# Three transformer blocks on one Trainium2 core: 1/rms moved to GpSimd, and the start of the kernel loaded in quarters

## The reference

```python
def rmsnorm(x, g, eps=1e-6):
    y = x * lax.rsqrt(jnp.mean(x * x, axis=-1, keepdims=True) + eps)
    return y * g

def swiglu(h, w_up, w_down):                 # 1024 -> 2 x 2816 -> 1024
    gate, up = jnp.split(h @ w_up, 2, axis=-1)
    return (jax.nn.silu(gate) * up) @ w_down

# first model, layers i = 0, 1 (the mixer is multiscale pooling, then differential attention)
    x = x + 0.5 * swiglu(rmsnorm(x, norm_g[i, 0]), ffn_w_up[i, 0], ffn_w_down[i, 0])
    h = rmsnorm(x, norm_g[i, 1])
    x = x + mixer(h) @ w_out                 # with attention over the memory, whose k, v come from rmsnorm(mem)
    x = x + 0.5 * swiglu(rmsnorm(x, norm_g[i, 2]), ffn_w_up[i, 1], ffn_w_down[i, 1])
  x = rmsnorm(x, final_norm_g)
# second model, one layer
    mix = mixer2(rms_norm(x, g_pre_mix)) @ w_out          # block attention and retention
    x = x + rms_norm(mix, g_post_mix)
    c = cross_attention(rms_norm(x, g_pre_cross), rms_norm(mem_2, g_mem))
    x = x + rms_norm(c, g_post_cross)
    f = (silu(gate) * up) @ w_down                        # of rms_norm(x, g_pre_ffn)
    x = x + rms_norm(f, g_post_ffn)
```

## Time and profile before

| What | us |
|---|---|
| median of 3 runs (1547.17 to 1547.46) | 1547.34 |
| the profiled execution, its own time | 1548.35 |
| its span, first to last instruction | 1546.6 |
| PE busy, share of the span | 1469.9, 95% |
| DVE busy | 880.9, 57% |
| ACT busy | 723.5, 47% |
| POOL busy | 5.1, 0% |
| DMA, moved 262.07 MB | mean 169 GB/s |

### The profile page before, as it was taken

One profiled execution on the slowest core, in us unless ns is written; L12 is line 12 of the kernel. 1 busy time (PEld: TensorE's weight loads), 2 busy tenths in 40 slices (PEclk: granted clock), 3 DMA queues, 4 the chain that ended last, 5 costly groups with the idle time before them and its releaser, 6 DMA issues.

```text
span 1546.6 us, 18695 instructions
## 1 busy us (share of the span) xinstructions
PE 1469.9 (95%) x7412; PEld 1237.0 (80%) x7412; DVE 880.9 (57%) x1001; ACT 723.5 (47%) x928; POOL 5.1 (0%) x13
## 2 busy tenths in 40 slices
PE   5999998999999999999989899999998899899997
PEld 4888898988888888888876688888877688788886
DVE  4555567655455654546668665445766655555444
ACT  5454453445434644445445555435433643444443
POOL 0000000000000000000000000000000000000000
PEclk9999999999999999999999899999999899999999
DMA  9555553445555455555323355554523353345551
GB/s 384 193 188 184 178 188 118 166 152 204 189 188 183 163 214 190 177 188 182 136 82 109 136 185 204 184 191 161 177 110 109 129 184 136 123 163 190 191 190 55
DMA packets 36846, 262.07 MB, mean 169 GB/s; under 512 B 4096, under 2 KB 4224, under 8 KB 5536
## 3 DMA queue, kind: packets, MB, share of 16 engines
q1 hardware_dynamic: 35568, 254.53, 46.7%
q0 software_dynamic: 1200, 6.42, 1.0%
HBM read 259.88 MB, written 1.05 MB: 169 GB/s over the span
## 4 chain that ended last, share of the span: by engine, by line
PE 85%; DVE 8%; ACT 5%; issue 1%; DMA 1%; DVEq 0%; SPq 0%; ACTq 0%
PE prod L864 14%; PE prod L866 14%; PE prod L865 14%; PE acc L864 9%; PE acc L865 9%; PE acc L866 9%; PE prod L858 4%; PE prod L859 4%; PE prod L860 4%; DVE w_lo L1288 2%; PE aux L894 2%; ACT w_hi L1106 1%; DVE sq L1566 1%; ACT four L1239 1%; DVE small L1372 1%
## 5 line engine op out<-in xcount | busy, mean ns | idle before, releaser
L1288 DVE TENSOR_TENSOR w_lo<-raw,w_hi 128x2048 fp32r<-128x2048 f32 x238 | 544.9, 2291 | 333.8 <-ACT w_hi L1106 333.4
L1106 ACT CAST w_hi<-raw 128x2048 fp32r<-128x2048 f32 x238 | 453.4, 1907 | 233.5 <-PE acc L866 154.7
L864 PE MATMUL prod<-w_hi,acts_h 128*128 128x512 f32 x944 | 376.1, 398 | 16.9 <-DVE w_lo L1288 13.5
L866 PE MATMUL prod<-w_hi,acts_l 128*128 128x512 f32 x944 | 369.5, 391 | 0.0
L865 PE MATMUL prod<-w_lo,acts_h 128*128 128x512 f32 x944 | 368.8, 391 | 0.0
L864 PE MATMUL acc<-w_hi,mix_h 128*128 128x512 f32 x600 | 240.2, 400 | 3.5 <-DVE mix_l L1581 2.5
L865 PE MATMUL acc<-w_lo,mix_h 128*128 128x512 f32 x600 | 235.9, 393 | 0.0
L866 PE MATMUL acc<-w_hi,mix_l 128*128 128x512 f32 x600 | 235.7, 393 | 0.0
L864 PEld LDWEIGHTS prod<-w_hi,acts_h 128*128 128x128 f32 x944 | 178.2, 189 | 54.5 <-DVE w_lo L1288 17.0
L866 PEld LDWEIGHTS prod<-w_hi,acts_l 128*128 128x128 f32 x944 | 178.0, 189 | 38.4
L865 PEld LDWEIGHTS prod<-w_lo,acts_h 128*128 128x128 f32 x944 | 178.5, 189 | 35.4 <-issue 0.2
(11 more groups left out here) (178 smaller groups left out, 1215.6 us busy)
## 6 DMA issues: line engine op xcount, KB each, us to landing
raw<-in_weights_dram SPq DMA_DIRECT2D x238, 1024.0 KB, 4.9
work<-in_mem_dram POOLq DMA_DIRECT2D x2, 1024.0 KB, 9.0
grow<-in_gain_rows_dram POOLq DMA_DIRECT2D x4, 512.0 KB, 3.6
tabs<-in_tabs_dram SPq DMA_DIRECT2D x1, 1697.0 KB, 14.8
work<-in_x_t_dram SPq DMA_DIRECT2D x2, 512.0 KB, 6.5
x_res<-in_x_dram SPq DMA_DIRECT2D x1, 1024.0 KB, 11.3
work<-in_mem_t_dram POOLq DMA_DIRECT2D x1, 1024.0 KB, 7.6
obuf<-in_mem_t_dram POOLq DMA_DIRECT2D x1, 1024.0 KB, 7.9
```

The lines of the kernel that those rows point to most:

```text
L864: pe.matmul(out, still_hi, wh, start=first, stop=False, skip_group_check=True)
L866: return pe.matmul(out, still_lo, wh, start=False, stop=last, skip_group_check=True)
L1106: act.copy(w_hi[:, c % RING], raw[:, c % RAW]).then_inc(hi_done, 1)
L1288: dve.tensor_tensor(w_lo[:, c % RING], raw[:, c % RAW], w_hi[:, c % RING].bitcast(F32), ALU.subtract).then_inc(lo_done, 1)
```

## The change

1. **1/rms on POOL.** The `stat` items leave ACT and DVE. POOL adds the halves, scales and adds eps, and raises to the power -0.5; each of its operations waits for the one before by a semaphore. The sums of squares get a second buffer. In the double norm POOL has six operations in a row, and DVE's scaling of x becomes an item of its own, `scale_x`, two chunks later.
2. **The start in quarters.** x transposed comes in quarters of 256 KB, chunks 0, 1 and 2 in quarters of 256 KB each, all from SP in the order of need; ACT and DVE split them quarter by quarter. Of `tabs` only the first 258 columns (identity, ones, eps) come from SP at the start; the other 3136 are issued by POOL after the first statistic and the first chunk.
3. **PE's first chunk** does both halves of the tokens for each quarter (`first_chunk`), after six matmuls on zeros that a memset of POOL's allows.
4. **ACT's first instruction** is a Silu of one column, which loads its table.

The core of the diff:

```diff
+        def quarter(k):
+            return slice(k * 512, (k + 1) * 512)
@@ block.sync
-            sp.dma_start(q_t[:, 0:4], A["x_t"][:, 0:4]).then_inc(xt_loaded[0], 16)
-            sp.dma_start(raw[:, 0], weights[0]).then_inc(raw_loaded[0], 16)
-            sp.dma_start(q_t[:, 4:8], A["x_t"][:, 4:8]).then_inc(xt_loaded[1], 16)
-            sp.dma_start(raw[:, 1], weights[1]).then_inc(raw_loaded[1], 16)
+            for c in range(2):
+                for k in range(4):
+                    if k % 2 == 0:
+                        kt = 4 * c + k
+                        sp.dma_start(q_t[:, kt:kt + 2], A["x_t"][:, kt:kt + 2]).then_inc(xt_loaded[kt // 2], 16)
+                    sp.dma_start(raw[:, c, quarter(k)], weights[c][:, quarter(k)]).then_inc(piece_loaded[c][k], 16)
             sp.dma_start(x[:], A["x"]).then_inc(x_loaded, 16)
-            sp.dma_start(tabs[:], A["tabs"]).then_inc(tabs_loaded, 16)
-            sp.dma_start(raw[:, 2], weights[2]).then_inc(raw_loaded[2], 16)
+            for k in range(4):
+                sp.dma_start(raw[:, 2, quarter(k)], weights[2][:, quarter(k)]).then_inc(piece_loaded[2][k], 16)
+            sp.dma_start(tabs[:, 0:FIRST_TABLES], A["tabs"][:, 0:FIRST_TABLES]).then_inc(tabs_loaded, 16)
@@ block.gpsimd
-            pool.wait_ge(chunk_used, 1)
+            pool.memset(mem_v[:, 0, 0:512], 0.0).then_inc(ready, 1)
+            def statistic(it):
+                n, r = it["n"], rstd[it["slot"]]
+                if it["of"] == "y":
+                    pool.wait_ge(y_squared, it["y_squared"])
+                else:
+                    pool.wait_ge(squared, plan.squares[n])
+                own(pool.tensor_tensor(ms, ss[n % 2][:, :, 0], ss[n % 2][:, :, 1], ALU.add))
+                if it["of"] == "xf":
+                    own(pool.tensor_tensor(ms, ms, rstd["one"], ALU.mult))
+                    own(pool.tensor_tensor(ms, ms, rstd["one"], ALU.mult))
+                own(pool.tensor_scalar(root, ms, 1.0 / D, 1e-6, ALU.mult, ALU.add))
+                if it["of"] == "xf":
+                    own(pool.tensor_tensor(root, root, minus_half, ALU.pow))
+                    pool.tensor_tensor(r, root, rstd["one"], ALU.mult).then_inc(rstd_done, 1)
+                else:
+                    pool.tensor_tensor(r, root, minus_half, ALU.pow).then_inc(rstd_done, 1)
+                if kind == "stat":
+                    statistic(it)
+                    if it["n"] == 0:
+                        pool.wait_ge(chunk_used, 1)
+                        pool.dma_start(tabs[:, FIRST_TABLES:], A["tabs"][:, FIRST_TABLES:]).then_inc(late_tabs_loaded, 16)
+                        ... (lambda, mem_t, mem and grow, as before)
@@ block.tensor
+            def first_chunk(it):
+                for k in range(4):
+                    pe.wait_ge(acts_lo, k + 1)
+                    piece_ready(0, k)
+                    for t in range(2):
+                        mm = token_passes(prod_flat[t], 0, k * 512, acts_h[:, k, tokens(t)], acts_l[:, k, tokens(t)],
+                                          k == 0, False)
+                mm.then_inc(chunk_used, 1)
+            pe.wait_ge(ready, 1)
+            for _ in range(6):
+                pe.matmul(aux[:, 0:S], mem_v[:, 0, 0:P], mem_v[:, 0, S:2 * S], start=True, stop=True)
@@ block.scalar
+            def split_piece(c, k):
+                act.wait_ge(piece_loaded[c][k], 16)
+                act.copy(w_hi[:, c, quarter(k)], raw[:, c, quarter(k)]).then_inc(hi_done if k == 3 else piece_hi, 1)
+            act.wait_ge(ready, 1)
+            act.activation(mem_v[:, 1, 0:1], mem_v[:, 0, 0:1], ACT.Silu)
-                elif kind == "stat":
-                    act.wait_ge(ms_done, it["n"] + 1)
-                    act.activation(root, ms, ACT.Sqrt, bias=eps_col[0], scale=1.0 / D).then_inc(rooted, 1)
@@ block.vector
-                elif kind == "stat":
-                    ... (the adds, products and reciprocals)
+                elif kind == "scale_x":
+                    dve.wait_ge(xf_done, 4)
+                    dve.wait_ge(rstd_done, it["stat"])
+                    for t in range(2):
+                        ins = dve.tensor_scalar(x[:, t], x[:, t], rstd["one"][:, t:t + 1], None, ALU.mult)
+                    own(ins)
```

More of the change, by code:

```diff
@@ L519, in make_plan @@
     pl.project(w, 512, "k", 0)
+    pl.add("scale_x", stat=pl.stat)
     pl.rope("q", 0, "moba", pl.read - 1)
@@ L717, in build @@
         vecs_loaded = sem("vecs_loaded")
-        xt_loaded = [sem(f"xt_loaded{n}") for n in range(2)]
+        piece_loaded = [[sem(f"piece_loaded{c}{k}") for k in range(4)] for c in range(RAW)]
+        piece_hi = sem("piece_hi")
+        piece_lo = sem("piece_lo")
+        ready = sem("ready")
+        xt_loaded = [sem(f"xt_loaded{n}") for n in range(4)]
         x_loaded = sem("x_loaded")
         tabs_loaded = sem("tabs_loaded")
+        late_tabs_loaded = sem("late_tabs_loaded")
         lam_loaded = sem("lam_loaded")
@@ L854, in _, with piece_ready @@
             pending = []
+            def piece_ready(c, k):
+                if k < 3:
+                    pe.wait_ge(piece_lo, 3 * c + k + 1)
+                else:
+                    pe.wait_ge(lo_done, c + 1)
             def column_passes(out, slot, a, moving_hi, moving_lo, first, last):
@@ L923, in tokens_chunk @@
                         if seen[of] < it["acts"] and t == 0:
-                            pe.wait_ge(ready, it["acts"] - KT + kt + 1)
+                            pe.wait_ge(lo_done_of, it["acts"] - KT + kt + 1)
+                        if it["c"] in (1, 2) and t == 0:
+                            piece_ready(it["c"], k)
                         mm = token_passes(prod_flat[e % 2], slot, k * 512, hi[:, base + kt, tokens(t)],
@@ L1112, in flush, with square @@
                     state["split"] += 1
-            def square(source, b):
+            def square(source, b, n):
                 t, cols = piece(b)
-                return act.activation(unread[b], source, ACT.Square, accum_out=ss[:, t, b // 2:b // 2 + 1])
+                if b == 0 and n >= 2:
+                    act.wait_ge(rstd_done, n - 1)
+                return act.activation(unread[b], source, ACT.Square, accum_out=ss[n % 2][:, t, b // 2:b // 2 + 1])
             def acts_pair(it, bank):
@@ L1167, in _ @@
                         t, cols = piece(b)
-                        ins = square(x[:, t, cols], b)
+                        ins = square(x[:, t, cols], b, 0)
                     ins.then_inc(squared, 1)
-                    act.wait_ge(tabs_loaded, 16)
+                    for k in range(4):
+                        split_piece(2, k)
+                    state["split"] = RAW
                 elif kind == "prep":
@@ L1283, in _ @@
         def _(dve):
-            state = {"split": 0, "target": RING, "own": 0, "ms": 0}
+            state = {"split": 0, "target": RING, "own": 0}
             def split(c):
@@ L1289, in split, with split_piece @@
                                   ALU.subtract).then_inc(lo_done, 1)
+            def split_piece(c, k):
+                if k == 3:
+                    dve.wait_ge(hi_done, c + 1)
+                else:
+                    dve.wait_ge(piece_hi, 3 * c + k + 1)
+                dve.tensor_tensor(w_lo[:, c, quarter(k)], raw[:, c, quarter(k)], w_hi[:, c, quarter(k)].bitcast(F32),
+                                  ALU.subtract).then_inc(lo_done if k == 3 else piece_lo, 1)
             def flush(upto=None):
@@ L1446, in _ @@
                                                  ).then_inc(acts_lo, 1)
-                        if kt == 3:
-                            flush(1)
-                    flush(2)
+                        split_piece(kt // 4, kt % 4)
+                    for k in range(4):
+                        split_piece(2, k)
+                    state["split"] = RAW
                 elif kind == "prep":
                     if it["resid"] == "post":
+                        dve.wait_ge(rstd_done, it["n"])
                         for b in range(4):
@@ L1483, in _ @@
                                                  op0=ALU.mult, op1=ALU.subtract).then_inc(mem_lo, 1)
[L1484 to L1503 removed]
+                elif kind == "scale_x":
+                    dve.wait_ge(xf_done, 4)
+                    dve.wait_ge(rstd_done, it["stat"])
+                    for t in range(2):
+                        ins = dve.tensor_scalar(x[:, t], x[:, t], rstd["one"][:, t:t + 1], None, ALU.mult)
+                    own(ins)
                 elif kind == "store":
+                    dve.wait_ge(rstd_done, plan.stat)
                     for b in range(4):
@@ L1630, in number @@
                 n["squared"] += 1
+            else:
+                it["y_squared"] = 4 * n["row"]
             plan.squares[it["n"]] = n["squared"] if it["of"] != "y" else None
```

91 lines of the change are left out of this document (39 added, 52 removed).

## The result

The changed kernel takes 1551.48 us (median of 15 runs) against 1547.34: ratio 1.0024, 95% interval 1.0016 to 1.0032. One of the 15 runs took 1676.2 us, with a granted clock of 0.84 in place of 0.97, and is left out of every ratio; the median of the other 14 is 1551.11. The kernel is slower: the interval excludes 1, and 0.24% is just beyond the 0.2% that the prediction had named. I had forecast 1546.4 and a range up to 1550.0. The profiled execution took 1551.48, its span is 1549.7, 3.1 us longer than before.

The account below looks back on a forecast made before the run. PE, busy for 95% of the span, was taken as the bound. Start -1.6, double norm +0.2, cross attention +1.0 and end -0.5 sum to -0.9 us: 1547.34 to 1546.4 (chance 0.38), range 1544.5 to 1550.0.

Parts of the forecast that it names:

- The start, -1.6: PE's restart behind chunk 3 at 25.84 instead of 28.84, less 1.4 us lost to the clock: 1.6 us gained.
- the term of the packets: At the start, smaller packets delay chunk 3's landing by 0.8 us (0 to 1.6), from 20.26 to 21.06.
- The price of an operation: POOL on 128x2: 0.30 us per add or scaling, 0.60 for the power, 0.04 per handover; three operations 1.30.
- The double norm, +0.2: At the double norm, products start 0.87 us earlier and POOL's six operations take 2.4: +0.2 us (-1.4 to +2.1).
- Rival 1: Double norm: POOL's add waits for DVE's split unless it starts before 1087; +1.7 us, 1547.9; chance 0.28.
- After the cross attention, +1.0: POOL's statistic waits behind its DMA of the next grow; DVE starts late: +1.0 us (+0.1 to +2.4).
- The end, -0.5: Behind the last matmul, 1/rms at 1540.75 instead of 1541.25: -0.5 us (-1.4 to +0.9).
- Rivals 2 and 3: 2: POOL's small operations dear, mean 0.75 us, 1551.0, chance 0.10; 3: first statistic 2 us late, 1548.4, chance 0.06.
- Rival 5: The start gives nothing because the quarters land no earlier: 1548.0, chance 0.08.
- four signs of being wrong: Restart before 24; three POOL operations over 2 us; double-norm spread over 1.5 us later; PE gap at an unnamed place.

Follow-up runs that it names:

- split_held: Changed kernel with VectorE's split of the next chunk at the double norm held back until 1/rms is done: 1548.56 us, ratio 1.0002 to the kernel before.
- before_longer: Kernel before with six small unused VectorE additions in the chain ahead of the double norm's spread: 1551.71 us, ratio 1.0023 to the kernel before.
- norm_warm: Changed kernel with nine matmuls nobody reads ahead of the double norm's spread: 1547.64 us, ratio 1.0004 to the kernel before.
- gain_behind: Changed kernel with GpSimd's DMA of the next gain row behind the statistic instead of ahead: 1549.52 us, ratio 1.0014 to the kernel before.
- both: Changed kernel with VectorE's split held until 1/rms at the double norm and the gain row's DMA behind the statistic: 1545.67 us, ratio 0.9984.
- filled: Changed kernel with 14 more matmuls on zeros ahead of PE's wait for chunk 2 at the start: 1548.97 us, ratio 1.0009.
- best_warm: Changed kernel with the repairs of both, first silu ahead of chunk 3's split, and 5, 7 and 7 unread matmuls in three PE waits: 1538.2 us, ratio 0.9944.

## Why the prediction was wrong, by its steps

- **The start, -1.6.** PE's first matmul (7.00 for 7.5), chunk 3 as the bound, the 4.7 us behind it, a wait of some 8 us (7.17) and 1.4 us lost to the clock were right. What was wrong is the term of the packets: 0.8 us, at most 1.6. Chunk 3 landed at 22.67, against 20.26 if packets had no price: they cost 2.4 us. So the restart came at 27.34 instead of 25.84, and the 1.5 us that it is ahead of the earlier trace rows go back to the clock: at the wait near 269 the changed kernel is 0.1 us ahead. By medians the start is worth nothing here (1.0021 without it, 1.0024 with it). So the term came to -0.1 instead of -1.6.
- **The price of an operation** held: 0.28 from start to start for add and scaling (0.34 taken), 0.79 for the power (0.64), 1.35 for the three (1.30).
- **The double norm, +0.2: here the prediction failed.** It took for granted that GpSimd's six operations run beside VectorE's split of the next chunk. The wait grew by 1.08, and Rival 1 was the mechanism, which I had put second. GpSimd's add started at 1086.63, in the midst of the split, and ended with it. I had put the decision on whether it starts before 1087, and by that Rival 1 would be out; the wait shows in its length. split_held changes nothing but the split's place, and the add is short again. The Trainium skill (SBUF — State Buffer, "Who interferes with whom") says that a VectorE instruction with two SBUF inputs contends with a GpSimd one that reads SBUF, and the traces agree: 1.30 us beside the split, 0.21 without it.
- **What neither the forecast nor any rival had**: the clock behind a longer wait at the double norm. I took it into account where a wait of 2.6 us became one of 8, but not where 3.5 became 4.6. There it cost about 2.2 us more than the wait itself, up to 75 us later; before_longer shows it without GpSimd, and norm_warm shows it gone when PE is kept busy. With it, the double norm is +3.2 instead of +0.2. Without it Rival 1's 1547.9 would have been within the range; this term and the start's 1.5 us are what took the time out of it.
- **After the cross attention, +1.0**: the wait grew by 1.22, by the mechanism given: the DMA ahead of the statistic cost 1.6 us (gain_behind), and GpSimd's own three operations gave 0.4 of it back against the root. Behind it about 0.6 us came back in the stretch up to the end, in both profiles. By medians taking the DMA away gains 0.10% without the other repair and 0.18% with it.
- **The end, -0.5**: -0.4 measured.
- **Rivals 2 and 3** are out: the twelve operations on the path took 0.41 us in the mean, the stretched add among them, and the first add at 19.83 took 0.19, so no first call showed in it. The Trainium skill (GPSIMD Engine Reference, "Instruction dispatch") gives about 6 us for a first call of a freshly loaded kernel; no run here shows it on the path. Rival 5 came true for the start's gain, near nothing, but not in its cause: the quarters did land earlier.
- **The signs.** None of the four signs of being wrong that the prediction named showed: the restart is at 27.34 and not before 24, three operations take 1.3 us, the spread is 0.86 us later, and no new gap of PE's stands elsewhere. They look at waits and at GpSimd's prices, and the largest loss lies in stretches in which PE is busy nearly all the time.

What stays open: why the loss from 1141 to 1164 depends on a wait 50 us earlier, and why it has three levels; and why the one profile of both had it with a short wait. The range was too narrow at its upper end because its cases held single prices and no clock behind them.

## What to carry to other kernels

- Before work goes from VectorE to GpSimd, look which VectorE instructions with both inputs in SBUF can stand beside it; on a path that PE waits for, hold those back, and put no DMA issue ahead of it in GpSimd's queue.
- A microsecond more of PE's waiting cost three or four in this kernel. Price a wait with the clock of the stretch behind it, and where it can't be shortened, try matmuls that nobody reads: filled (by the least, 0.15%), norm_warm and best_warm were each faster than the same kernel without them.
- Where two kernels differ by a few tenths of a per cent, read two profiles of each before a stretch is explained.

## What of the hardware was not expected

- GpSimd's 128x2 add ends with VectorE's split in all eight places of the changed kernel's trace where it starts beside one: 0.05 us behind it, after 0.7 to 2.07 us, where it takes 0.19 to 0.21 alone. From the timelines of the changed kernel, of GpSimd and of VectorE:

```profile
207.16 0.71 POOL L859 TENSOR_TENSOR stats<-stats 128x2 f32<-128x2 f32 x1 [110.31 <-ACT sq L1188]
207.96 0.19 POOL L863 TENSOR_SCALAR stats<-stats 128x2 f32<-128x2 f32 x1
...
1234.24 2.07 POOL L859 TENSOR_TENSOR stats<-stats 128x2 f32<-128x2 f32 x1
```

```profile
205.54 2.28 DVE L1363 TENSOR_TENSOR w_lo<-raw,w_hi 128x2048 fp32r<-128x2048 f32 x1
207.85 1.66 DVE L1389 SCALAR_TENSOR_TENSOR acts_l<-acc,vecs,acts_h 128x256 fp32r<-128x256 f32 x4
...
1233.97 2.29 DVE L1363 TENSOR_TENSOR w_lo<-raw,w_hi 128x2048 fp32r<-128x2048 f32 x1 [0.57 <-ACT w_hi L1176]
```

  Ends: 207.87 and 207.82, 1236.31 and 1236.26. The scaling at 207.96 runs in 0.19 beside VectorE's instruction that reads PSUM and SBUF.
- At the end of the kernel the root with its table load and the reciprocal took 1.82 us up to VectorE's adds; GpSimd's add, scaling and power took 1.43 from ScalarE's last square (1542.93), 0.4 less.
- 256 KB pieces, 2 KB a partition, moved at 299 GB/s with the DMA engines 95% busy, where 4 and 8 KB a partition gave 426: 103 ns for a packet of 2 KB, 310 for one of 8 KB.
